# Experts' sums as products of 64 by 64 on opposite quarters of TensorE's array, in two accumulators

## The reference

```python
g = softmax(best)                                  # (token, head, 16)
a = gelu(einsum('pd,phkd->phk', hb, u_tab[expert]))
w = g * a
y = einsum('phk,phkd->pd', w, v_tab[expert])       # 128 rows of 1024 per token
```

## Time and profile before

| what | value |
|---|---|
| median of the runs | 2941.03 us |
| span of the profiled execution | 2932.5 us (the page gives no other time of it) |
| PE busy | 2492.6 us, 85% |
| DVE, ACT, POOL busy | 1624.7, 1064.4, 843.4 us |
| DMA | 918.88 MB, of which 805.36 MB are the gathers |
| chain that ended last | DMA 44%, PE 40%, ACT 7%, DVE 6% |
| L1513 (sums) | 3072 passes, 1509.2 us busy |

### The profile page before, as it was taken

One profiled execution on the slowest core, in us unless ns is written; L12 is line 12 of the kernel. 1 busy time (PEld: TensorE's weight loads), 2 busy tenths in 40 slices (PEclk: granted clock), 3 DMA queues, 4 the chain that ended last, 5 costly groups with the idle time before them and its releaser, 6 DMA issues.

```text
span 2932.5 us, 23875 instructions
## 1 busy us (share of the span) xinstructions
PE 2492.6 (85%) x7216; PEld 1140.0 (39%) x7216; DVE 1624.7 (55%) x3860; ACT 1064.4 (36%) x3055; POOL 843.4 (29%) x796
## 2 busy tenths in 40 slices
PE   7998889898777789899778988979789998777777
PEld 2453553644222244344222323335457543222222
DVE  1042551666667766666666655431553676667764
ACT  2132440343433344433433333332441444343333
POOL 0100000244434443344333433310000444444342
PEclk9999979999999999999999999999899999999999
DMA  6233002699999999999999999942003999999998
GB/s 254 83 116 115 30 1 72 278 421 421 421 421 397 421 421 421 389 422 421 421 421 392 421 421 421 421 174 83 21 1 138 422 421 421 421 392 421 421 421 331
DMA packets 127313, 918.88 MB, mean 313 GB/s; under 512 B 14160, under 2 KB 15440, under 8 KB 15696
## 3 DMA queue, kind: packets, MB, share of 16 engines
q0 software_dynamic: 110592, 805.36, 66.3%
q1 hardware_dynamic: 15152, 102.69, 9.2%
q10 hardware_dynamic: 1440, 9.32, 0.8%
HBM read 916.25 MB, written 1.05 MB: 313 GB/s over the span
## 4 chain that ended last, share of the span: by engine, by line
DMA 44%; PE 40%; ACT 7%; DVE 6%; issue 3%; POOL 0%; ACTq 0%; SPq 0%; POOLq 0%; PEldq 0%; DVEq 0%
DMA regA<-uv_dram,idx 44%; PE bank L1513 14%; PE bank L1238 5%; PE bank L1436 3%; DVE regA L1104 3%; PE bank L1461 3%; PE bank L1202 2%; PE bank L1524 2%; PE bank L1248 1%; PE bank L1179 1%; PE bank L1358 1%; ACT sqreg L732 1%; PE bank L1394 1%; PE bank L1165 1%; PE bank L1298 1%
## 5 line engine op out<-in xcount | busy, mean ns | idle before, releaser
L1513 PE MATMUL bank<-regA,sqreg 128*128 128x512 f32 x3072 | 1509.2, 617 | 308.2 <-ACT sqreg L732 265.6
L386 POOL DMA_INDIRECT regA<-uv_dram,idx x768 | 820.8, 1069 | 1931.9 <-PE bank L1513 1134.7
L1104 DVE SCALAR_TENSOR_TENSOR regA<-regA,regB 128x1024 f32<-128x1024 f32 x768 | 941.4, 1226 | 700.9 <-DMA regA<-uv_dram,idx 699.9
L1513 PEld LDWEIGHTS bank<-regA,sqreg 128*128 128x128 f32 x3072 | 535.1, 190 | 1108.6 <-ACT sqreg L732 651.0
L728 ACT ACTIVATE regB<-regB 128x1 f32<-128x1 f32 x768 | 155.5, 202 | 1150.9 <-DVE regA L1104 1150.5
L732 ACT ACTIVATE sqreg<-con,regB 128x128 f32<-128x128 f32 x768 | 308.3, 401 | 25.2
L729 ACT ACTIVATE regB<-regB 128x1 f32<-128x1 f32 x768 | 226.2, 295 | 25.0
L1461 PE MATMUL bank<-hT,wring 128*128 128x256 f32 x768 | 214.9, 389 | 11.3 <-ACT hT L686 11.3
L1461 PEld LDWEIGHTS bank<-hT,wring 128*128 128x128 f32 x768 | 148.1, 196 | 141.1 <-issue 130.9
L1238 PE MATMUL bank<-hT,wring 128*128 128x512 f32 (+2 forms) x384 | 147.9, 543 | 12.5 <-ACT hT L426 9.4
L1238 PEld LDWEIGHTS bank<-hT,wring 128*128 128x128 f32 (+1 forms) x384 | 71.1, 191 | 88.5 <-issue 77.7
(11 more groups left out here) (206 smaller groups left out, 1867.6 us busy)
## 6 DMA issues: line engine op xcount, KB each, us to landing
wring<-w_dram SPq DMA_DIRECT2D x96, 1024.0 KB, 6.9
regA<-uv_dram,idx POOLq DMA_INDIRECT x768, 15.3
mlaw<-uq_dram ACTq DMA_DIRECT2D x2, 1152.0 KB, 8.5
...
```

The lines of the kernel that those rows point to most:

```text
L386: g.indirect_dma_start(ring[:, s, :], None, uv_tabs[l], bass.IndirectOffsetOnAxis(idx[:, i % 2, k:k + 1], 0)).then_inc(landed[s], 16)
L1104: v.scalar_tensor_tensor(out=ring[:, s, 0:D], in0=ring[:, s, 0:D], scalar=1.0, in1=hrow[:, i % 2, :], op0=ALU.mult, op1=ALU.mult, accum_ou ...
L1513: mm = p.matmul(acc[:, f * 512:f * 512 + 512], diag[:, m % DIAGS, :], ring[:, s, D + f * 512:D + f * 512 + 512], start=(m % P == 0), stop= ...
```

## The change: what it does

The slots are taken in pairs. For an even slot tokens 0 to 63 use rows and columns 0 to 63 of the array and tokens 64 to 127 rows and columns 64 to 127; the even slot adds up in `acc` (banks 6 and 7) with tokens in their places. An odd slot's two halves take the two other quarters and add up in `bank45` with upper and lower tokens exchanged. So `diag` is now 128x64, two diagonals of 64, and a pair is 8 products of 64 by 64 by 512 columns. Both slots of a pair are marked as used by its last product. Banks 4 and 5 are taken for good, so `sums_out` makes two copies, the turn of a tile's sums adds `yrow[0]` times the identity and `yrow[1]` times an identity with its halves exchanged, and both kinds of turns go through bank 3, in two halves that wait for each other (`hr_ready`, and the new signal `x_part`). The constants grow by 128 columns.

```diff
@@ -90,14 +90,16 @@
...
 
-C_ID, C_ONE = 0, 128
-C_MASK = 256
+HALF = P // 2
+C_ID, C_ONE = 0, P + HALF
+C_MASK = C_ONE + P
 C_INV = C_MASK + DIRS * 2 * 256
...
 C_IOTA = C_DIR + 2
-CB = C_IOTA + 16
+C_TWO = C_IOTA + 16
+CB = C_TWO + HALF
 
@@ -128,6 +130,7 @@
...
         ps += [bank45[:, 0:512], bank45[:, 512:1024], acc[:, 0:512], acc[:, 512:1024]]
+        both_acc = (acc, bank45)
 
@@ -157,7 +160,7 @@
...
         ring = shaped(regA, 0, RING, 2 * D)
-        diag = shaped(sqreg, 0, DIAGS, P)
+        diag = shaped(sqreg, 0, DIAGS, HALF)
 
@@ -199,8 +202,8 @@
...
         keysA = shaped(regB, 4176, 2, 4, PKEYS)
-        yrow = regB[:, 5200:6224]
-        modrow = shaped(regB, 7168, 2, WT)[0:2]
+        yrow = shaped(regB, 5200, 2, D)
+        modrow = shaped(regB, 7824, 2, WT)[0:2]
         uqw = shaped(mlaw, 0, 3, 768)
@@ -209,6 +212,8 @@
...
         ident = con[:, C_ID:C_ID + P]
+        swapped = con[:, C_ID + HALF:C_ID + HALF + P]
+        two64 = con[:, C_TWO:C_TWO + HALF]
         ones = con[:, C_ONE:C_ONE + P]
@@ -312,6 +317,7 @@
...
         yt_mm = signal("yt_mm", 2 * NT[0], 2 * NT[1])
+        x_part = signal("x_part", 2 * NT[0], 2 * NT[1])
         x_done = signal("x_done", *NT)
@@ -709,11 +715,11 @@
...
 
-                def rows_in(i):
-                    a.wait_ge(hr_mm.sem, hr_mm.at(l, i + 1))
+                def rows_in(i, f):
+                    a.wait_ge(hr_mm.sem, hr_mm.at(l, 2 * i + f + 1))
                     if i >= 2:
                         a.wait_ge(dotted.sem, dotted.at(l, (i - 1) * SLOTS))
-                    a.activation(hrow[:, i % 2, :], bank45[:, :], ACT.Copy).then_inc(hr_ready.sem, 1)
+                    a.activation(hrow[:, i % 2, f * 512:f * 512 + 512], ps[3][:, :], ACT.Copy).then_inc(hr_ready.sem, 1)
 
@@ -729,14 +735,15 @@
...
                         a.wait_ge(v_used.sem, v_used.at(l, m - DIAGS + 1))
-                    a.activation(diag[:, m % DIAGS, :], ident, ACT.Copy, scale=coef[:, n:n + 1]).then_inc(diag_ready.sem, 1)
+                    a.activation(diag[:, m % DIAGS, :], two64, ACT.Copy, scale=coef[:, n:n + 1]).then_inc(diag_ready.sem, 1)
 
...
                         a.wait_ge(yt_mm.sem, yt_mm.at(l, 2 * i))
-                    a.activation(yrow, acc[:, :], ACT.Copy).then_inc(y_ready.sem, 1)
+                    a.activation(yrow[:, 0, :], acc[:, :], ACT.Copy)
+                    a.activation(yrow[:, 1, :], bank45[:, :], ACT.Copy).then_inc(y_ready.sem, 1)
 
@@ -745,7 +752,8 @@
...
                 keys(0)
-                rows_in(0)
+                rows_in(0, 0)
+                rows_in(0, 1)
                 for n in (1, 2, 3):
@@ -772,8 +780,8 @@
...
                             sums_out(i - 1)
-                        if n == 6 and r == 2 and i + 1 < nt:
-                            rows_in(i + 1)
+                        if n in (6, 10) and r == 2 and i + 1 < nt:
+                            rows_in(i + 1, n // 10)
                         if l == 0 and i == 3 and n % 4 == 3 and n < 24:
@@ -1099,7 +1107,7 @@
...
                     if n == 0 and Q % QUADS == 0:
-                        v.wait_ge(hr_ready.sem, hr_ready.at(l, i + 1))
+                        v.wait_ge(hr_ready.sem, hr_ready.at(l, 2 * i + 2))
                     v.wait_ge(landed[s], 16 * (at // RING + 1))
@@ -1110,9 +1118,10 @@
...
                         k = 4 * f + j
-                        link(v.scalar_tensor_tensor(out=xT[:, k, t * P:(t + 1) * P], in0=ps[4 + f][:, j * P:(j + 1) * P],
+                        link(v.scalar_tensor_tensor(out=xT[:, k, t * P:(t + 1) * P], in0=ps[3][:, j * P:(j + 1) * P],
                                                     scalar=gate_f[:, k, s:s + 1], in1=xT[:, k, t * P:(t + 1) * P],
                                                     op0=ALU.mult, op1=ALU.add))
+                    v.sem_inc(x_part.sem, 1)
                     if f:
@@ -1480,39 +1489,45 @@
...
 
-                def rows_turn(i):
+                def rows_turn(i, f):
                     t = TILES[l][i]
-                    if i == 0:
+                    if i == 0 and f == 0:
                         p.wait_ge(x_mid.sem, x_mid.at(l, KC))
                         p.wait_ge(h_ready.sem, h_ready.at(l, 2 * KC))
-                    if i == 1:
-                        p.wait_ge(hr_ready.sem, hr_ready.at(l, 1))
-                    if i >= 2:
+                    if i == 1 or f:
+                        p.wait_ge(hr_ready.sem, hr_ready.at(l, 2 * i + f))
+                    if i >= 2 and f == 0:
                         p.wait_ge(x_done.sem, x_done.at(l, i - 1))
-                    for k in range(KC):
-                        mm = p.transpose(bank45[:, k * P:(k + 1) * P], hT[:, k, t * P:(t + 1) * P], ident)
+                    for j in range(4):
+                        mm = p.transpose(ps[3][:, j * P:(j + 1) * P], hT[:, 4 * f + j, t * P:(t + 1) * P], ident)
                     mm.then_inc(hr_mm.sem, 1)
 
-                def sums_turn(i):
-                    p.wait_ge(y_ready.sem, y_ready.at(l, i + 1))
-                    p.wait_ge(hr_ready.sem, hr_ready.at(l, min(i + 2, nt)))
-                    if i:
-                        p.wait_ge(x_done.sem, x_done.at(l, i))
-                    for f in range(2):
-                        for j in range(4):
-                            mm = p.transpose(ps[4 + f][:, j * P:(j + 1) * P], yrow[:, (4 * f + j) * P:(4 * f + j + 1) * P], ident)
-                        mm.then_inc(yt_mm.sem, 1)
+                def sums_turn(i, f):
+                    if f == 0:
+                        p.wait_ge(y_ready.sem, y_ready.at(l, i + 1))
+                        p.wait_ge(hr_ready.sem, hr_ready.at(l, 2 * min(i + 2, nt)))
+                    if i or f:
+                        p.wait_ge(x_part.sem, x_part.at(l, 2 * i + f))
+                    for j in range(4):
+                        k = 4 * f + j
+                        p.matmul(ps[3][:, j * P:(j + 1) * P], yrow[:, 0, k * P:(k + 1) * P], ident, start=True, stop=False)
+                        mm = p.matmul(ps[3][:, j * P:(j + 1) * P], yrow[:, 1, k * P:(k + 1) * P], swapped, start=False, stop=True)
+                    mm.then_inc(yt_mm.sem, 1)
 
...
 
-                    s = gather_at(l, m) % RING
                     if m % P == 0 and m:
                         p.wait_ge(y_ready.sem, y_ready.at(l, m // P))
-                    p.wait_ge(diag_ready.sem, diag_ready.at(l, m + 1))
+                    p.wait_ge(diag_ready.sem, diag_ready.at(l, m + 2))
                     for f in range(2):
-                        mm = p.matmul(acc[:, f * 512:f * 512 + 512], diag[:, m % DIAGS, :], ring[:, s, D + f * 512:D + f * 512 + 512],
-                                      start=(m % P == 0), stop=(m % P == P - 1))
-                    mm.then_inc(v_used.sem, 1)
+                        for e in range(2):
+                            s = gather_at(l, m + e) % RING
+                            for u in range(2):
+                                o = HALF * (u ^ e)
+                                mm = p.matmul(both_acc[e][o:o + HALF, f * 512:f * 512 + 512], diag[HALF * u:HALF * u + HALF, (m + e) % DIAGS, :],
+                                              ring[HALF * u:HALF * u + HALF, s, D + f * 512:D + f * 512 + 512],
+                                              start=(m % P == 0), stop=(m % P == P - 2))
+                    mm.then_inc(v_used.sem, 2)
 
@@ -1546,10 +1561,10 @@
...
                             scores(now)
-                    if r == 0 and i and n == 8:
-                        sums_turn(i - 1)
-                    if r == 2 and i + 1 < nt and n == 4:
-                        rows_turn(i + 1)
+                    if r == 0 and i and n in (8, 18):
+                        sums_turn(i - 1, n // 18)
+                    if r == 2 and i + 1 < nt and n in (4, 8):
+                        rows_turn(i + 1, n // 8)
                     if l == 0 and i == 3:
@@ -1567,20 +1582,22 @@
...
                     if n == 0:
-                        rows_turn(0)
+                        rows_turn(0, 0)
+                        rows_turn(0, 1)
                 for Q in range(nq + 1):
...
                             aside(Q, n)
-                        if 0 <= m < P * nt:
-                            values(m)
+                        if 0 <= m < P * nt and m % 2:
+                            values(m - 1)
 
...
     con = np.zeros((P, CB), np.float32)
-    con[:, C_ID:C_ID + P] = np.eye(P)
+    con[:, C_ID:C_ID + P + HALF] = np.concatenate([np.eye(P), np.eye(P)[:, :HALF]], axis=1)
+    con[:, C_TWO:C_TWO + HALF] = np.tile(np.eye(HALF), (2, 1))
     con[:, C_ONE:C_ONE + P] = 1.0
```

4 lines of the change are left out of this document (2 added, 2 removed).

## The result

The changed kernel took 2957.95 us (median of 4 runs, 2951.54 to 2962.78), 1.0053 times the kernel before (interval 1.0036 to 1.0071). A second series of 8 runs gave 2953.42 us and 1.0046 (1.0029 to 1.0063). A few executions in the chip's slower state (one of experiment 2, at 3302 us, the others of the kernel before) are left out of all medians and ratios. The forecast of 2953.3 us, slower by 0.4%, holds in sign and size. Two of its reasons do not: the tile changes cost nothing over a whole retrieval, and the clock, rival 4 with a chance of 0.08, fell.

The account below looks back on a forecast made before the run. DMA was taken to bound the kernel within a tile. Ends 9.0, changes of tile 3.2 and constants 0.1 sum to 12.3 us on a span of 2932.5; with 8.5 carried over, 2953.3 us, range 2943 to 2967.

Parts of the forecast that it names:

- tile changes: Four changes of tile in the expert retrieval: second copy delays the first products, +0.8 us each, 3.2 in all.
- rival 4: TensorE, less busy, drops to clock 0.50 in the tail: pair and both turns double, 6.2 us an end, 2966; chance 0.08.
- What bounds the kernel: Expert retrieval inside a tile: DMA is full at 421 or 422 GB/s, share 1.01; TensorE, 79% busy, is not the bound.
- A pair on TensorE: Sums of two slots, 16 passes of 64x512: 2.2 us taken, near full overlap of the four quarters.
- Rivals 1 and 2: Pair of slots on TensorE: 3.7 us if column halves take turns (chance 0.15), 7.2 us with no overlap (chance 0.03).
- Late release of the even slot: Ring of 8 in the retrieval: even slot freed 2.49 us later, four gathers stay outstanding; priced at nothing.
- Rival 1: Column halves take turns: 10 us more over ends, changes of tile and starts, 2963; hidden within a tile; chance 0.15.
- The ends: Serial chain with DMA empty where each of two layers ends: +4.5 us each from pair, copy and turns, 9.0 in all.
- deeper dips in the four slices: Sign to look for: bandwidth dips in the four slices holding the changes of tile get a little deeper.
- Two starts: Start of each layer's retrieval: 1.9 us of delays fit in 2.8 us of slack; nothing, up to +2 each.
- gaps of 2.8 us only: Argument against a falling clock: TensorE's pauses would be only 2.8 us, while clock 0.50 was seen after idling 9 us.

Follow-up runs that it names:

- experiment 2: Changed kernel with each product of the sums issued twice, so the experts' sums come out doubled; 2970.57 us, 1.0104 times the kernel before.
- experiment 5: Kernel before, with the sums of two slots issued together and both slots freed together, products still 128 by 128 in one accumulator; 2954.32 us, ratio 1.0041.
- experiment 7: Kernel before with a second copy of the tile's sums ahead of the signal; 2947.85 us, 1.0021 times the kernel before.
- experiments 1: Changed kernel with odd slots in the same quarters of the array as even ones, still with the second accumulator; 2969.14 us, 1.0097 times the kernel before.

## Why the prediction was right, point by point

- **What bounds the kernel.** Right: in a tile 421 GB/s, DMA share 1.01, before and after, while TensorE's busy time fell by 391 us (2492.6 to 2101.6).
- **A pair on TensorE: 2.2 us taken.** It is 1.95 to 1.99. Rivals 1 and 2 are refuted: 3.67 us is what a pair takes when odd and even slots use the same two quarters. The rule on row tiles in one PSUM bank (Trainium skill, "TensorEngine Tiling (Array Packing)", PSUM Pressure) does not hold back disjoint partitions here. The prediction put a pair by that rule at 7.2 us, which is too much: the two halves of a slot would take turns, but even and odd slots write different banks, so 3.7 us, two at a time, is what the rule alone asks; the measured 1.95 is below that too.
- **Late release of the even slot: nothing.** Right in sum, for a reason the prediction did not give. Four outstanding gathers suffice inside a tile only. Where the ring is refilled, pairing costs, 10.7 us in the whole retrievals with 3.7 us pairs (experiment 5); with fast pairs nothing of it is left in the sum. Rival 1's 10 us came to 14 in the retrieval and 3 in the ends against a changed kernel at full clock.
- **The ends: 4.5 us each.** At full clock 13.5 less 9.1 is 4.4: pair 0.0 for 0.2, copy 0.9 for 1.0, turn of half 0 1.4 for 1.3, half 1 2.1 for 2.1. This is the step that carried the forecast. What it lacked is the clock: the four ends measured have 4.4 to 9.6 us more than before, mean 7.4.
- **Four changes of tile: +3.2.** Wrong in the sum; measured over whole retrievals +0.5 and -1.0 in layer 0, -0.6 and -0.5 in layer 1, starts included. The price is there at the changes themselves (0.8 to 2.0 for the 12 slots around each, 0.8 forecast), and the second copy costs its 0.7 a change (experiment 7). It comes back elsewhere in the retrieval, which the prediction did not have. That two places freed at once and pairs of 2 us do this is likely from experiments 1 and 5, but no run shows it alone. The sign that the prediction named, deeper dips in the four slices, told nothing: from 421 they add up to 118 in the first profile and 105 in the second, for 114 before.
- **Two starts: nothing.** Right within the same numbers; the ninth gather comes 24.0 and 25.3 us after the first, for 23.9.
- **Rival 4, the clock, 0.08.** It happened. The argument "gaps of 2.8 us only" was wrong: where TensorE pauses 3 us after a fast pair, the next pair runs at the lower clock. Its price, 6.2 us an end if both turns and the pair run at half, is nearly met in the longest of the four ends, 5.2 us over 13.5 (pair and both turns, some 1.75 each); in the other three the clock was full for all or part of the chain.
- **Sum.** Forecast 12.3. Measured: ends 14.0 to 15.4, retrieval 0.0 to -1.6, in all 12.5 to 15.4, beside medians 13.6 and 17 us apart. The tile changes were 3.2 to 4.8 us too dear, and the clock, left out of the sum, cost 2.7 to 3 us an end. That these two errors nearly cancel is luck, and so is part of the closeness of the number; the direction and the bulk of it come from the chain at the ends.

What stays open is how much the lower clock moves the mixer of layer 1. It took 329.9 and 332.5 us after for 325.3 before, but 332.0 in two kernels of the old family with a clock of 1.00 in the tiles, so nothing is shown. Open too is why the clock fell in the turns of one end and not of another with the same steps before it.
